# Second mixer of a hybrid decoder trunk: first convolution tap and norm squares on ScalarE, convolution one piece later, step size folded into the tokens, scores of four heads in one product

## The reference

```python
z, xbc, dt = split(u @ w_in)                       # 4096, 6144 and 64 columns
xbc = silu(causal_dwconv(xbc, conv_w, conv_b))     # 4 taps
xs, Bm, Cm = split(xbc)                            # 64 heads x 64, 8 groups x 128 twice
dt = softplus(dt + dt_bias); A = -exp(a_log)
X = xs * dt;  A_cs = cumsum(A * dt) within chunks of 128 tokens
y  = (C B^T * exp(segsum(A dt))) X                 # inside a chunk
   + C (B^T (exp(A_cs[-1] - A_cs) X)) exp(A_cs)    # from the chunk before
y  = (y + d_skip * xs) * silu(z)
y  = y * rsqrt(mean over each group's 512 channels of y*y + eps) * norm_g
return y @ w_out
```

## Time and profile before

| | us |
|---|---|
| median of 3 runs | 2788.56 |
| lowest and highest of them | 2776.84 to 2804.09 |
| span of the profiled execution | 2772.1 |
| own time of the profiled execution | not given; the lowest run is 4.7 above its span |
| stage B1 with its parts in B2, first half | about 1198 to 1482 of the span |
| the same, second half | about 1556 to 1840 of the span |

### The profile page before, as it was taken

The page is one execution under the profiler, slowest core; times in us unless marked ns, Lnnn a source line. Parts: engine busy times, 40 slices in busy tenths (PEclk is TensorE's granted clock), DMA queues, the critical chain, the costliest instruction groups (busy, mean ns, idle before and its releaser), DMA issues.

```text
span 2772.1 us, 50755 instructions
## 1 busy us (share of the span) xinstructions
PE 2698.1 (97%) x17359; PEld 2436.3 (88%) x17359; DVE 2087.2 (75%) x2979; ACT 1307.9 (47%) x1762; POOL 440.5 (16%) x474
## 2 busy tenths in 40 slices
PE   7998999999999999999999999999999999999997
PEld 5887888888888888999998999988888888888897
DVE  8988876765676677888896788978767556767776
ACT  5565344444444444445563455644444444444443
POOL 4444210000000111211111011122000000001122
PEclk9999999999999999999999999999999999999999
DMA  5555565656666565555555655555665666665654
GB/s 189 167 164 159 183 196 182 192 178 190 199 190 195 189 190 166 176 180 172 176 181 161 198 168 168 183 159 181 198 187 187 180 199 193 186 194 176 189 179 149
DMA packets 158369, 502.33 MB, mean 181 GB/s; under 512 B 17792, under 2 KB 20160, under 8 KB 157120
## 3 DMA queue, kind: packets, MB, share of 16 engines
q1 hardware_dynamic: 158192, 501.04, 58.1%
q10 hardware_dynamic: 80, 0.07, 0.0%
HBM read 498.88 MB, written 2.16 MB: 181 GB/s over the span
## 4 chain that ended last, share of the span: by engine, by line
PE 81%; DVE 12%; issue 3%; ACT 1%; POOL 1%; DMA 1%; DVEq 0%; SPq 0%; ACTq 0%; POOLq 0%
PE bank L382 41%; PE bank L384 21%; PE bank L365 6%; PE bank L366 6%; PE bank L367 6%; DVE wlo L797 3%; DVE arena L948 2%; DVE arena L946 1%; ACT whi L572 1%; DVE arena L942 1%; DVE arena L1021 0%; PE bank L540 0%; DVE arena L1110 0%; DVE R L854 0%; DVE rinvh L838 0%
## 5 line engine op out<-in xcount | busy, mean ns | idle before, releaser
L382 PE MATMUL bank<-R,whi 128*128 128x512 f32 x5504 | 1931.2, 396 | 36.3 <-DVE R L854 13.3
L797 DVE TENSOR_TENSOR wlo<-wraw,whi 128x1024 fp32r<-128x1024 f32 (+3 forms) x1056 | 1190.4, 1137 | 521.7 <-ACT whi L572 519.5
L384 PE MATMUL bank<-R,wlo 128*128 128x256 f32 x5504 | 1540.1, 280 | 0.0
L572 ACT ACTIVATE whi<-wraw 128x1024 fp32r<-128x1024 f32 (+3 forms) x1056 | 991.8, 947 | 923.8 <-PE bank L384 772.6
L382 PEld LDWEIGHTS bank<-R,whi 128*128 128x128 f32 x5504 | 1036.7, 188 | 281.9 <-DVE wlo L797 16.4
L384 PEld LDWEIGHTS bank<-R,wlo 128*128 128x128 f32 x5504 | 1043.5, 190 | 0.1
L365 PE MATMUL bank<-R,whi 128*128 128x256 f32 x1856 | 535.1, 288 | 15.4 <-DVE wlo L797 12.9
L366 PE MATMUL bank<-R,whi 128*128 128x256 f32 x1856 | 526.4, 284 | 0.0
L367 PE MATMUL bank<-R,wlo 128*128 128x256 f32 x1856 | 526.3, 284 | 0.0
L365 PEld LDWEIGHTS bank<-R,whi 128*128 128x128 f32 x1856 | 357.1, 192 | 23.6 <-DVE wlo L797 17.4
L366 PEld LDWEIGHTS bank<-R,whi 128*128 128x128 f32 x1856 | 357.2, 192 | 2.1 <-issue 1.9
(11 more groups left out here) (166 smaller groups left out, 1418.6 us busy)
## 6 DMA issues: line engine op xcount, KB each, us to landing
wraw<-in_F SPq DMA_DIRECT2D x352, 512.0 KB, 4.1
wraw<-in_B SPq DMA_DIRECT2D x224, 512.0 KB, 3.7
wraw<-in_A SPq DMA_DIRECT2D x96, 512.0 KB, 3.6
wraw<-in_F SPq DMA_DIRECT2D x128, 384.0 KB, 3.1
wraw<-in_F SPq DMA_DIRECT2D x128, 320.0 KB, 3.2
wraw<-in_PL SPq DMA_DIRECT2D x64, 320.0 KB, 3.2
wraw<-in_PL SPq DMA_DIRECT2D x64, 256.0 KB, 2.8
arena<-cs_rows SPq DMA_DIRECT2D x8, 1024.0 KB, 7.2
```

The costliest lines, as they stand in the source:

```text
L382: nc.tensor.matmul(dst.rearrange("p (s t) -> p s t", s=2), whi[:, q % RING, cols], src[:, :, k, :], start=first, stop=False)
L384: mm = nc.tensor.matmul(dst[:, 0:SEQ], wlo[:, q % RING, cols], src[:, 0, k, :], start=False, stop=last)
L572: nc.scalar.activation(whi[:, slot, 0:w * BLOCK], wraw[:, slot, 0:w * BLOCK], ACT.Copy).then_inc(w_hi, 1)
L797: V.tensor_tensor(wlo[:, slot, 0:w * BLOCK], wraw[:, slot, 0:w * BLOCK], whi[:, slot, 0:w * BLOCK].bitcast(F32), ALU.subtract).then_inc(w_ ...
```

## The change

- `conv` for the mixer is split. The first tap and the bias go to ACT (`ca = cpad * w3 + b`, Identity, at the same odd q as the eviction, behind a wait for it). The other three taps (`later_taps`) are issued by DVE one step later, at even q, tanh on ACT and silu on DVE another step later, at odd q from 3 to 13.
- The squares for the group norm go from four products on POOL to one ACT instruction over the four tiles, at q = 1 of the next group (or q = 0 of B2), behind a wait for all four.
- DVE makes `xtok` from PSUM already times dt (the ACT copies go); `xdec` multiplies by the decay alone; the product of decay and dt at q = 7 of the first group goes.
- The scores need no dt any more: two instructions over 128x1024 instead of sixteen over 128x128 in each group.

```diff
@@ ACT, stage B1, step q
-                            if q % 2 == 0 and 2 <= q <= 12:
+                            if q % 2 == 1 and 3 <= q <= 13:
                                 nt = q // 2 - 1
                                 act.wait_ge(conv_done, group * 6 + nt + 1)
                                 nc.scalar.activation(cth[:, nt % 2, :], ca[:, nt, :], ACT.Tanh).then_inc(conv_t, 1)
+                            if q % 2 == 1 and q < 12:
+                                nt = q // 2
+                                if nt == 0 and not very_first:
+                                    act.wait_ge(y_read, group * 4)
+                                act.wait_ge(bank_free, it * ph["groups"] + ph["group0"] + 4 + nt + 1)
+                                nc.scalar.activation(ca[:, nt, :], cpad[:, nt % 2, 3:3 + SEQ], ACT.Identity,
+                                                     bias=flat(bpar[:, at(group), nt * 5 + 4:nt * 5 + 5]),
+                                                     scale=flat(bpar[:, at(group), nt * 5 + 3:nt * 5 + 4])
+                                                     ).then_inc(tap_done, 1)
+                            if q == 1 and not first:
+                                y_square(group - 1)
...
-                            if q == 14:
-                                act.wait_ge(turned, group + 1)
-                                for c in range(2):
-                                    nc.scalar.activation(xtok[:, c, :], bank[5 + c][:], ACT.Copy).then_inc(xtok_done, 1)
...
+                def y_square(group):
+                    act.wait_ge(yz_done, group * 4 + 4)
+                    nc.scalar.activation(ysq, zt, ACT.Square).then_inc(ysq_done, 1)
@@ DVE, stage B1, step q
                             if q % 2 == 0 and 2 <= q <= 12:
                                 nt = q // 2 - 1
-                                dve.wait_ge(conv_t, group * 6 + nt + 1)
-                                V.scalar_tensor_tensor(out=ca[:, nt, :], in0=cth[:, nt % 2, :], scalar=1.0,
-                                                       in1=ca[:, nt, :], op0=ALU.add, op1=ALU.mult).then_inc(silu_done, 1)
+                                dve.wait_ge(tap_done, group * 6 + nt + 1)
+                                later_taps(cpad[:, nt % 2], ca[:, nt, :],
...
                                 V.tensor_tensor(cpad[:, nt % 2, 3:3 + SEQ], src, rinv[:], ALU.mult).then_inc(bank_free, 1)
-                                dve.wait_ge(bank_free, g0 + nt + 1)
-                                conv(cpad[:, nt % 2], ca[:, nt, :], par, par(4), None, conv_done)
+                            if q % 2 == 1 and 3 <= q <= 13:
+                                nt = q // 2 - 1
+                                dve.wait_ge(conv_t, group * 6 + nt + 1)
+                                V.scalar_tensor_tensor(out=ca[:, nt, :], in0=cth[:, nt % 2, :], scalar=1.0,
+                                                       in1=ca[:, nt, :], op0=ALU.add, op1=ALU.mult).then_inc(silu_done, 1)
...
+                                own.link(V.tensor_tensor(by_head(xtok[:, 0, :]), by_head(bank[5][:]), per_head(dtt[:, 0, heads]),
+                                                         ALU.mult))
+                                V.tensor_tensor(by_head(xdec), by_head(xtok[:, 0, :]), per_head(wdt[:, heads]),
                                                 ALU.mult).then_inc(xdec_done, 1)
+                                own.mark(V.tensor_tensor(by_head(xtok[:, 1, :]), by_head(bank[6][:]), per_head(dtt[:, 1, heads]),
+                                                         ALU.mult))
...
+                                V.tensor_tensor(csb[:, h0:h0 + 4, :], csb[:, h0:h0 + 4, :],
+                                                cbm.rearrange("p c l -> p (c l)").rearrange("p (e n) -> p e n", e=1)
+                                                .broadcast_to([P, 4, SEQ]), ALU.mult).then_inc(sc_done, 1)
@@ POOL, y_square
-                        for j in range(4):
-                            pool.wait_ge(yz_done, group * 4 + j + 1)
-                            G.tensor_tensor(ysq[:, j, :], zt[:, j, :], zt[:, j, :], ALU.mult).then_inc(ysq_done, 1)
-
-                        pool.wait_ge(ysq_done, group * 4 + 4)
+                        pool.wait_ge(ysq_done, group + 1)
```

More of the change, by code:

```diff
@@ L564, in _, with flat @@
             own = Chain(act, act_own)
+            def flat(x):
+                return x.rearrange("p a t -> p (a t)")
             def hi(ph_piece, q, w, early=False):
@@ L946, in conv, with later_taps @@
                     own.link(V.tensor_scalar(dst, pad[:, 3:3 + SEQ], taps(3), bias, ALU.mult, ALU.add))
+                    later_taps(pad, dst, taps, done)
+                def later_taps(pad, dst, taps, done):
                     for k in (2, 1):
@@ L1100, in body @@
                                 nt = q // 2 - 1
-                                dve.wait_ge(conv_t, group * 6 + nt + 1)
-                                V.scalar_tensor_tensor(out=ca[:, nt, :], in0=cth[:, nt % 2, :], scalar=1.0,
-                                                       in1=ca[:, nt, :], op0=ALU.add, op1=ALU.mult).then_inc(silu_done, 1)
+                                dve.wait_ge(tap_done, group * 6 + nt + 1)
+                                later_taps(cpad[:, nt % 2], ca[:, nt, :],
+                                           lambda k, nt=nt, group=group: flat(bpar[:, at(group), nt * 5 + k:nt * 5 + k + 1]),
+                                           conv_done)
                             if q % 2 == 1:
@@ L1124, in body, with by_head, per_head @@
                                                          .broadcast_to([P, 2, CHUNK]), ALU.mult))
-                                own.link(V.tensor_copy(btok, bank[4][:, 256:384]))
-                                dve.wait_ge(xtok_done, group * 2 + 1)
-                                V.tensor_tensor(xdec.rearrange("p (e c) -> p e c", e=GROUP_HEADS),
-                                                xtok[:, 0, :].rearrange("p (e c) -> p e c", e=GROUP_HEADS),
-                                                wdt[:, at(group * GROUP_HEADS, GROUP_HEADS)]
-                                                .rearrange("p (e c) -> p e c", c=1).broadcast_to([P, GROUP_HEADS, 64]),
+                                own.mark(V.tensor_copy(btok, bank[4][:, 256:384]))
+                                def by_head(x):
+                                    return x.rearrange("p (e c) -> p e c", e=GROUP_HEADS)
+                                def per_head(x):
+                                    return x.rearrange("p (e c) -> p e c", c=1).broadcast_to([P, GROUP_HEADS, 64])
+                                heads = at(group * GROUP_HEADS, GROUP_HEADS)
+                                own.link(V.tensor_tensor(by_head(xtok[:, 0, :]), by_head(bank[5][:]), per_head(dtt[:, 0, heads]),
+                                                         ALU.mult))
+                                V.tensor_tensor(by_head(xdec), by_head(xtok[:, 0, :]), per_head(wdt[:, heads]),
                                                 ALU.mult).then_inc(xdec_done, 1)
+                                own.mark(V.tensor_tensor(by_head(xtok[:, 1, :]), by_head(bank[6][:]), per_head(dtt[:, 1, heads]),
+                                                         ALU.mult))
                             if q in (15, 17):
@@ L1136, in body @@
                                     own.need(own.latest())
-                                for e in range(h0, h0 + 4):
-                                    for c in range(2):
-                                        s = V.scalar_tensor_tensor(
-                                            out=csb[:, e, c * CHUNK:(c + 1) * CHUNK], in0=csb[:, e, c * CHUNK:(c + 1) * CHUNK],
-                                            scalar=dtt[:, c, at(group * GROUP_HEADS + e)], in1=cbm[:, c, :],
-                                            op0=ALU.mult, op1=ALU.mult)
-                                s.then_inc(sc_done, 1)
+                                V.tensor_tensor(csb[:, h0:h0 + 4, :], csb[:, h0:h0 + 4, :],
+                                                cbm.rearrange("p c l -> p (c l)").rearrange("p (e n) -> p e n", e=1)
+                                                .broadcast_to([P, 4, SEQ]), ALU.mult).then_inc(sc_done, 1)
                 def z_silu(group, j):
@@ L1172, in group_norm @@
                                                in1=grms[:], op0=ALU.mult, op1=ALU.mult).then_inc(yn_done, 1)
-                steps(dve, ph, body, own, {"A1": 26, "B1": 25, "F1": 6, "PL": 0}.get(name, 4))
+                steps(dve, ph, body, own, {"A1": 26, "B1": 21, "F1": 6, "PL": 0}.get(name, 4))
                 own.close()
```

16 lines of the change are left out of this document (6 added, 10 removed).

## The result

| | before | after |
|---|---|---|
| median of the runs | 2790.0 us (4 runs) | 2851.39 us (4 runs) |
| lowest and highest | 2776.84, 2804.09 | 2842.95, 2859.52 |
| profiled execution: time, span | not given, 2772.1 | 2857.72, 2856.0 |
| stage B1 with B2 | 647.3 us | 717.2 us |
| of it PE busy, PE idle | 629.7, 17.6 | 652.8, 64.4 |

The account below looks back on a forecast made before the run. PE, busy 97% of the span, was taken as the bound. Waits of 47.6 us plus 15 for the clock less 2.6 gave 60 us, so 2849 us on the median of 2788.6; range 2800 to 2880.

Parts of the forecast that it names:

- the mechanism: In B1, ACT's hi stands behind the tap that waits for DVE's eviction; new PE waits of 5 to 9 us, chance 0.68.
- The rival "faster": In B1, DVE stays the bound with a 4.55 us cycle and wlo waits go: -9.5 us, 2779 us; chance 0.07.
- The condition that I gave it: For "faster", the sixth eviction must be less than 0.5 us late, needing a cycle of about 4.3 us.
- The cycle: From one eviction to the next in B1, a chain over ACT and DVE of 5.65 us instead of 5.00.
- What stands in it: Squares, ebc, group_var, group_norm and POOL's loss between first and sixth evictions: sixth eviction 7.6 us late.
- The term that was mis-sized: DVE's loss where POOL works at the same time, per group: 2.0 us, bounds 0 and 3.6.
- From the sixth eviction to C B^T: The way from a group's sixth eviction to its sixth silu, needed by PE for C B^T: 8.0 us.
- The waits: PE waiting for the silu: 7.1 us in each of six groups, 3.6 and 1.4 in two others, 47.6 in all.
- the wait for the sum: PE's wait in B2 for the sum of squares, shortened by 1.3 us in each half: -2.6 us.
- The clock: PE running slower behind seven waits of 3 us or more, 2.2 us each: 15 us.
- Tokens and scores: From q = 14 on, where PE waits for nobody: no effect, at most 1 us in a group.
- Squares: One ACT instruction replacing POOL's four in B2: -2.6 us, bounds 0 and -3.2; on ACT in B1, 0.95 in the chain.

Follow-up runs that it names:

- number 1: Changed kernel, but in B1 ACT issues the hi of even steps 2 to 12 ahead of the preceding odd step's first tap: median 2763.65 us, ratio 0.9957.
- number 6: Kernel before plus only the token and score part (dt folded into tokens, scores of four heads in one product): stage 648.6 us against 647.3.
- number 5: Kernel before plus only the group-norm squares as one ACT instruction: stage 641.0 us, median 2779.64 us, ratio 0.9974.
- number 3: Changed kernel with the first tap back on DVE behind the eviction, convolution delay kept: stage 666.9 us, median 2804.38 us, ratio 1.0097.

## Why the prediction was right

- **The direction, the mechanism and the size hold:** 2851.39 measured, 2849 predicted; number 1 shows the mechanism. The rival "faster", with DVE as the bound, describes number 1 and not the kernel as written: the `hi` of the even steps on the wrong side of the tap and of what follows it decides between them. It came out at 0.43% below before where I had reckoned 9.5 us, 0.34%. The condition that I gave it was too strict: in number 1 the sixth eviction of the last group came 3.3 us late (32.05 against 28.8) and PE hardly waited, because the way from there to C B^T was 5.6 us and not the 8.0 of the slow chain.
- **The cycle.** Predicted 5.65 us between evictions, measured 5.75 in a cycle with nothing else in it (second half, first group). The 0.1 is the tap: 0.60 long and 0.51 to the next instruction, where I took 0.40 from a Copy. So even the bare chain gains nothing on PE's 5.76.
- **What stands in it.** From the first to the sixth eviction of the last group it took 38.4 us (1434.27 to 1472.67) where the terms give 36.4. `group_var` came as priced (2.1); `group_norm` was 1.6 instead of 2.1. The term that was mis-sized is POOL's: 0.7 beside the additions of the squares, 1.75 beside `y_split`, 1.44 beside `ce`, together 3.9 us against the 2.0 that I took and over my upper bound of 3.6. I had hoped that part of it would fall into DVE's waits; the waits were where I said, and POOL's work fell on the `lo` and the taps behind them.
- **From the sixth eviction to C B^T** 8.0 was predicted and 8.13 measured.
- **The waits.** For the last group 7.1 us were predicted, and C B^T came 9.1 us late: 8.1 of standing still (1.49, 2.11 and 4.52), and 1.0 in which it was slower without standing still. That is not the clock, which was granted in full from 1434 to 1476 (1.00). Some 0.7 lies around the three waits, whose idle time leaves out part of the gap (at the second, two matmuls start 2.39 us apart, the next one 0.22 behind, where 0.12 is usual, and 2.11 count as idle); 0.3 is the norm's own sum on PE. The loop groups wait 8.2 to 9.4 where the prediction has 7.1 beside the 1.7 that was there before, the last group of the second half 6.7 (predicted 7.1). First group 4.0 (predicted 3.6), and 0.7 more than before for a bank, as the third eviction was not on time as I had it; first of the second half 1.8 (predicted 1.4). B2: the wait for the sum is gone, net -2.8 (predicted -2.6). All told PE stands still 46.8 us longer; the prediction has 47.6 - 2.6 = 45.0.
- **The clock** was too low: 15 us predicted, 23.1 measured as slower matmuls. I counted one stretch of slow clock for each of seven waits. They brought 34.1 us at half speed, which is at most 17 us of loss, near my 15. What I left out is that three of the shorter waits ahead of piece 13 brought theirs too (10.2 us at half speed). In all it is 44.8 us more than before.
- **Why it still agrees.** The stage grew by 69.9 us and not 60, all of it in the terms above but for the 1.5 of chance at its beginning. The spans of the two profiled executions differ by 83.9, the medians by 61.4: they carry the spread of the rest of the program, which is as large as what was missed. The agreement to 2 us is luck; to 10 it is not.
- **Tokens and scores** cost and bring nothing (number 6); the 16 products take the 1.22 us predicted. **Squares** alone bring 6 us (number 5), more than my 2.6: the waits for `wlo` in the loop iterations are halved with them. This part I did not see because I priced them only inside the new chain.
- **What I had wrong after the prediction** came out in number 3, where I expected the delay alone to be almost free. It costs 27 us with this order on ACT, half of it as slower matmuls: a second `lo` and a wait for `hi` lie between the sixth eviction and its silu, and that eviction is late already. The prediction's sum held because its way from eviction to silu contained the delay; it went by the order of the instructions and not by a share for each part.

## What to carry to other kernels

When work moves to an engine with idle time, write down what stands behind it in that engine's order: if it waits for engine X and something X needs stands behind it, the two form a loop, and the busy shares (72% and 47% here) say nothing about it. Put the prefetch work ahead of the instruction that waits; here that turned +2.4% into -0.4%. Price a wait of PE above its length while PE is the bound, as each one also slows the matmuls behind it: here 23 us for 47 us of waiting.

## What the runs showed of the hardware

- Identity with a scale and a bias per partition took 602 ns for 256 fp32 columns, with the next instruction 0.51 us after its start; tanh of the same size 418 ns.
- A DVE instruction that meets POOL's `ce` loses most of the overlap: `lo` 2.67 instead of 1.22 beside a `ce` of 2.39, and 1.23 once `ce` was 0.47 long; a tap 2.63 instead of 0.41 (number 3). Beside the four shorter products of `y_split` DVE lost 1.75 of 3.3 us.
- Small matmuls in a wait of PE kept its clock up: 13 products in seven waits took the time at 1.2 GHz from 55.0 to 24.4 us and the stage from 717.2 to 705.7, some 10 us of it by their doing, though they are of no use to the result.
